# Odd layer's out projection: eight half-sized products become seven, with the sums of weight blocks made by transfers that add at their target

## The chip, the cores and the metric

The kernel runs on one core of one Trainium2 chip. The metric is the device time of one execution in microseconds (us); lower is better. Three runs of the kernel before stand at 1342.32, 1343.02 and 1346.22 us, median 1343.02.

## The reference, cut to what matters

Three transformer blocks run one after the other on 256 tokens of width 1024, all in f32: an even layer, an odd layer and a third block with 64 routed experts. The change touches the odd layer (index 1), from its attention outputs to the first layer norm:

```python
qf, kf, vf, fl = _split(x @ w_in_odd, ODD_SPLITS)
mix = forgetting_attention(hd(qf), hd(kf), hd(vf), fl, fox_f_bias) @ w_out_odd   # [256, 1024] @ [1024, 1024]
x = layer_norm(ALPHA * x + mix, ln_gain[1, 0], ln_bias[1, 0])
x = layer_norm(ALPHA * x + sqrelu_mlp(x, mlp_w_up[1], mlp_w_down[1]), ln_gain[1, 1], ln_bias[1, 1])
```

What is added up in `mix` must be the full product over all 1024 rows of `w_out_odd`.

## The kernel before, in words

Five engines run programs written out by hand, and semaphores order them. TensorE (`pe`) multiplies, VectorE (`dve`) takes products out of PSUM and normalises, ScalarE (`act`) does exponentials, square roots and copies, GpSimd (`pool`) issues a second stream of transfers and has a little arithmetic, and SyncE (`sp`) issues the stream of weights.

**Weights.** `d_stream` holds chunks of 1024 KB in the order of use. SyncE puts chunk n into slot n % 8 of `ring` as soon as chunk n - 8 is used (`s_used`, L675). The out projection's four chunks lie in slots 7, 0, 1 and 2. Each holds two row tiles of 128 rows by all 1024 columns. The first four chunks of the MLP behind it lie in slots 3 to 6, and its chunks 4 to 7 come into the slots 7, 0, 1, 2 once the out projection releases them.

**Out projection (`out_projection`, L984).** The attention outputs lie turned in `xT`: 8 tiles of 128 features by 256 tokens. Four quarters of the output (token tile t, column half) follow each other, each a sum of 8 matmuls 128x512 over the eight feature tiles, one PSUM bank each: 32 matmuls. Quarters 0 and 1 need token tile 0 of `xT` alone, quarters 2 and 3 need tile 1. Before the last quarter TensorE turns the normalised rows of token tile 0 (`turn_rows(x, "ln2", 0)`, L782).

**Residual (`residual`, L2333).** VectorE takes a quarter at a time, `y = ALPHA * x + ps`, and gathers its statistics (`half_stats`, L2256). After quarter 1 it normalises token tile 0 (`norm`, which is `layer_norm`, L2268 to L2274, with the square root by ScalarE) and then scales the context rows for the third block (`norm_context`, L2318 and L2323). After quarter 2 it copies half of the turned columns (`take_turn`, L2072) and makes two differences of MLP weight blocks (`other_differences`, L2503 and L2505). After quarter 3 it normalises token tile 1.

**MLP (`mlp(1)`).** Its up products begin with token tile 0's columns (L1002). In the middle of the second one TensorE turns the rows of token tile 1. It already uses seven products of halves in place of eight. Its down products (L1011) are each four matmuls 128x512, the same shape as a product of the change.

**GpSimd's queue** around the place, in order: gain and bias rows for both layer norms (`row`, L2972), a weight difference for the MLP (`first_difference`, L3008), the context load (L3148), a cleared row sum and three small bias loads (`start_sums`, L2993 and L2995), and two 1024 KB chunks of modulation weights (`start_mlp`, L3016), which VectorE reads during the MLP.

Of the kernel before, what the change touches and what calls it, by code (L numbers as in the profile page):

```python
# [19 lines left out]
ALU = mybir.AluOpType  # L20
# [28 lines left out]
HALF_SUMS = ODD_HALF + 4  # L49
DIFFS = ODD_DIFFS + 3 * 4  # L50
ADDED = ODD_ADDED + 3 * 6
TAKEN = ODD_TAKEN + 3

# [204 lines left out]
def build(nc, d_stream, d_params, d_consts, d_pool, d_x, d_ctx, d_gain, d_bias, d_ada, d_bada, d_final, d_out):  # L258
    with ExitStack() as ctx:
# [54 lines left out]
        s_fold = sem("fold_ready")  # L314
# [223 lines left out]
        def down_blocks(n0):  # L538

            chunks = [rows2(ring[:, (n0 + 4 + i) % RING, :]) for i in range(4)]  # L540
            return [[w[:, :, 512 * half:512 * (half + 1)] for w in chunks[2 * k:2 * k + 2]] for k in range(2) for half in range(2)]
        mod_sum = pairs[:].rearrange("p a b -> p (a b)")
# [227 lines left out]
        def _(pe):  # L770
# [177 lines left out]
            def mod_columns(n, tiles, bank):  # L948

                pe.wait_ge(s_fold, 1)  # L950
# [13 lines left out]
            def out_projection(n0, name, before_last):  # L964

                def wait_columns_of(t):
                    if name == "mix0":
                        wait_columns(name, t)
                    elif name == "mix1":
                        pe.wait_ge(s_odone, FIRST_TURNED + 2 * t + 2)  # L970
                    else:
                        pe.wait_ge(s_odone, FIRST_TURNED + 4 + t + 1)

                ws = [chunk(n0 + c).rearrange("p (k n) -> p k n", k=2) for c in range(4)]
                for q in range(4):
# [12 lines left out]
                    if q < 3:  # L988
                        mm.then_inc(s_quarter, 1)

            def mlp(layer, name, hook=None, before_last=None):
# [56 lines left out]
                def down(it, first=False, last=False):  # L1048
# [17 lines left out]
                    pe.wait_ge(s_y, it * 6 + (ADDED * layer + 1))  # L1066
# [3 lines left out]
                    pe.wait_ge(s_y, it * 6 + (ADDED * layer + 2))  # L1070
# [3 lines left out]
                    pe.wait_ge(s_y, it * 6 + (ADDED * layer + 3))  # L1074
# [72 lines left out]
            for c in range(2):  # L1147
# [7 lines left out]
                if c == 0:  # L1155
                    turn_hidden()
                    pe.wait_ge(s_fold, 1)
# [166 lines left out]
            out_projection(FIRST["out_odd"], "mix1", lambda: turn_rows(x, "ln2", 0))  # L1324
# [8 lines left out]
            pe.wait_ge(s_y, ADDED + ODD_ADDED)  # L1333
# [319 lines left out]
        def _(act):  # L1653
# [277 lines left out]
            for t in range(TT):  # L1931
                unread = (probT[:], hT[:, 0:4, :])[t].rearrange("p a b -> p (a b)")
# [126 lines left out]
        def _(dve):  # L2059
# [265 lines left out]
            def residual(section, before, norm, name, layer):  # L2325

                for q in range(4):
# [10 lines left out]
                    if q == 1 and layer == 1:  # L2338
                        norm_context()
                    if q == 2:  # L2340
                        take_turn(name, xT, only=0)
                        other_differences(layer)
# [28 lines left out]
            def mlp(layer, norm, hook=None, name=None):  # L2371
# [19 lines left out]
                def added(it, n):  # L2391
                    dve.wait_ge(s_y, it * 6 + (ADDED * layer + n))
# [99 lines left out]

            def other_differences(layer):
# [3 lines left out]
                if layer:  # L2497
                    dve.wait_ge(s_odone, FIRST_TURNED + 4)
                else:
                    dve.wait_ge(s_turn, TURN_AT["mix0"] + 4)  # L2500
                dve.wait_ge(s_full[(n0 + 2) % RING], 16 * ((n0 + 2) // RING + 1))
                dve.wait_ge(s_blk, 5 + layer)
# [823 lines left out]
```

## Time and profile before

| | before |
|---|---|
| median of 3 runs | 1343.02 us |
| the profiled execution's own time | 1343.69 us |
| its span in the profile | 1342.0 us |
| TensorE busy | 1319.2 us (98%) |
| VectorE busy | 678.5 us (51%) |
| ScalarE busy | 238.5 us (18%) |
| GpSimd busy | 95.8 us (7%) |
| out projection and its turn on TensorE | 487.15 to 515.60 us |
| moved from HBM | 356.88 MB, 267 GB/s over the span |

The profile is of one execution. Times count from the start of its span. The views used below are the page (totals and the chain of work that ended last), the timeline (instructions in order of time, neighbours of one kind merged), busy time by stretches, and the transfers with their time to landing. An f32 matmul of 128x512 shows as two records of 0.43 us each, so the 32 matmuls are 64 records. GpSimd's queue and SyncE's queue are served by the same 16 DMA engines.

### The profile page before, as it was taken

To read this page: it belongs to the slowest core of one execution; us is meant where nothing else is said; L and a number is where in the kernel's file an instruction comes from. 1 tells how busy PE (TensorE), PEld (TensorE's weight loads), DVE (VectorE), ACT (ScalarE), POOL (GpSimd) and SP (SyncE) were. 2 spreads that over 40 slices of the span, in tenths; PEclk is the share of its full clock that TensorE was granted. 3 is DMA by queue.
4 is the path that set the end of the run, shared out by engine and by line. 5 is a ranking of instruction groups with operands and counts; after the bars stand their busy time and mean duration, and the time that the engine had idled before them with its cause. 6 is when DMAs were issued, how large, how long until landed. Compare 5 with 4: busy or idle time off the path is not lost.

```text
span 1342.0 us, 19458 instructions
## 1 busy us (share of the span) xinstructions
PE 1319.2 (98%) x7520; PEld 821.6 (61%) x7520; DVE 678.5 (51%) x1261; ACT 238.5 (18%) x551; POOL 95.8 (7%) x116
## 2 busy tenths in 40 slices
PE   9999999999999999999999999999999999999996
PEld 8667585786789557588677666644444444444433
DVE  1235588877899549977887254322122122212213
ACT  2134321210220341120123152100000000000002
POOL 1125400000011030000000100000000000000001
PEclk9999999999999999999999999999999999999999
DMA  9930155555514445667664414499999999999994
GB/s 380 363 141 33 64 219 197 215 220 215 188 64 173 181 181 215 231 247 304 239 240 154 173 57 164 194 421 420 421 421 416 421 420 421 421 421 421 421 420 198
DMA packets 51072, 359.56 MB, mean 268 GB/s; under 512 B 5920, under 2 KB 6192, under 8 KB 8496
## 3 DMA queue, kind: packets, MB, share of 16 engines
q1 hardware_dynamic: 45312, 324.60, 60.1%
q0 software_dynamic: 5392, 32.05, 6.5%
q10 hardware_dynamic: 288, 1.80, 0.3%
q8 instruction: 56, 0.92, 0.3%
q14 instruction: 24, 0.20, 0.0%
HBM read 356.88 MB, written 1.05 MB: 267 GB/s over the span
## 4 chain that ended last, share of the span: by engine, by line
PE 91%; DVE 7%; issue 1%; ACT 0%; DVEq 0%; ACTq 0%
PE ps L1537 14%; PE ps L1011 13%; PE ps L1002 11%; PE ps L1566 7%; PE ps L1462 7%; PE ps L1515 7%; PE ps L984 5%; PE ps L819 4%; PE ps L1292 4%; PE ps L902 2%; PE ps L1285 2%; PE ps L923 2%; PE ps L824 1%; PE ps L858 1%; PE ps L1422 1%
## 5 line engine op out<-in xcount | busy, mean ns | idle before, releaser
L2845 DVE TENSOR_TENSOR masked_and_probs<-ps,gate_rows 128x512 f32<-128x512 f32 x52 | 33.5, 686 | 152.5 <-PE ps L1566 152.5
L1515 PE MATMUL ps<-masked_and_probs,probT 128*128 128x512 f32 x208 | 94.4, 594 | 0.9 <-DVE masked_and_probs L2845 0.9
L1462 PE MATMUL ps<-masked_and_probs,mix_rows 128*128 128x256 f32 (+1 forms) x416 | 93.0, 376 | 0.0
L1462 PEld LDWEIGHTS ps<-masked_and_probs,mix_rows 128*128 128x128 f32 x416 | 75.0, 190 | 28.8 <-issue 19.6
L1002 PEld LDWEIGHTS ps<-xT,ring 128*128 128x128 f32 x768 | 87.8, 192 | 3.8 <-issue 3.8
L1002 PE MATMUL ps<-xT,ring 128*128 128x128 f32 x768 | 88.7, 275 | 0.0
L1011 PE MATMUL ps<-ring,qk_tiles 128*128 128x512 f32 x192 | 85.2, 592 | 0.0
L984 PE MATMUL ps<-ring,xT 128*128 128x512 f32 x192 | 83.8, 593 | 0.0
L2833 DVE TENSOR_TENSOR masked_and_probs<-masked_and_probs,ps 128x256 f32<-128x256 f32 x26 | 11.0, 422 | 142.0 <-ACT masked_and_probs L2020 142.0
L1674 ACT ACTIVATE qk_tiles<-ps 128x512 f32<-128x512 f32 (+7 forms) x58 | 30.2, 522 | 246.2 <-PE ps L1002 238.5
L1537 PE MATMUL ps<-ring,vec_rows 128*32 128x512 f32 (+2 forms) x296 | 72.0, 592 | 0.0
L2020 ACT ACTIVATE masked_and_probs<-ps 128x256 f32<-128x256 f32 x26 | 10.0, 384 | 348.2 <-PE ps L1537 348.2
L1566 PE MATMUL ps<-ring,probT 128*32 128x512 f32 (+1 forms) x264 | 69.1, 596 | 0.1
L984 PEld LDWEIGHTS ps<-ring,xT 128*128 128x128 f32 x192 | 35.9, 190 | 42.9 <-issue 42.9
L1515 PEld LDWEIGHTS ps<-masked_and_probs,probT 128*128 128x128 f32 x208 | 37.2, 190 | 39.4 <-issue 39.1
L1011 PEld LDWEIGHTS ps<-ring,qk_tiles 128*128 128x128 f32 x192 | 35.8, 190 | 41.6 <-issue 41.1
L1002 PE MATMUL ps<-gate_rows,ring 128*128 128x128 f32 x512 | 59.9, 275 | 0.0
L1002 PEld LDWEIGHTS ps<-gate_rows,ring 128*128 128x128 f32 x512 | 58.4, 192 | 0.1
L1706 ACT ACTIVATE masked_and_probs<-masked_and_probs,negmax 128x128 f32<-128x128 f32 (+2 forms) x96 | 47.6, 497 | 59.4 <-DVE negmax L2232 52.1
L819 PE MATMUL ps<-xT,ring 128*128 128x256 f32 x240 | 52.7, 379 | 0.8 <-DVE xT L2072 0.8
L2357 DVE SCALAR_TENSOR_TENSOR masked_and_probs<-v_rows,csil,masked_and_probs 128x512 f32 (+1 forms) x64 | 48.0, 750 | 3.2 <-DMA v_rows<-in_ada 1.1
L819 PEld LDWEIGHTS ps<-xT,ring 128*128 128x128 f32 x240 | 45.2, 190 | 7.0 <-ACT xT L1662 1.0
(500 smaller groups left out, 2380.5 us busy)
## 6 DMA issues: line engine op xcount, KB each, us to landing
ring<-in_stream SPq DMA_DIRECT2D x200, 1024.0 KB, 9.7
qk_tiles<-in_stream SPq DMA_DIRECT2D x46, 1024.0 KB, 21.0
v_rows<-in_ada POOLq DMA_DIRECT2D x12, 1024.0 KB, 5.1
qk_tiles<-in_ada POOLq DMA_DIRECT2D x12, 1024.0 KB, 5.1
vec_rows<-in_stream SPq DMA_DIRECT2D x12, 1024.0 KB, 18.2
con<-in_stream SPq DMA_DIRECT2D x12, 1024.0 KB, 19.4
y_rows<-in_stream SPq DMA_DIRECT2D x12, 1024.0 KB, 20.4
par<-in_stream SPq DMA_DIRECT2D x12, 1024.0 KB, 21.1
```

The costliest lines, as they stand in the source:

```text
L819: mm = pe.matmul(ps[0:n, bank, off:off + T], w[:, kk, col:col + n], src[:, k, :], start=bank not in started, stop=k == KT - 1, skip_group_ ...
L984: mm = pe.matmul(ps[:, q, :], xT[:, k, t * P:(t + 1) * P], ws[k // 2][:, k % 2, half * 512:(half + 1) * 512], start=k == 0, stop=k == KT - 1)
L1002: mm = pe.matmul(ps[:, bank, m * P:(m + 1) * P], weights[:, kk, m * P:(m + 1) * P], tokens[:, kk, :], start=fresh and m == 0 and kk == 0, ...
L1011: mm = pe.matmul(ps[:, bank, :], hidden[:, kk, :], weights[kk // 2][:, kk % 2, :], start=fresh and kk == 0, stop=kk == 3, skip_group_check ...
L1292: mm = pe.matmul(ps[:, bank, m * P:(m + 1) * P], weights[:, kk, m * P:(m + 1) * P], tokens[:, kk, :], start=fresh and m == 0 and kk == 0, ...
L1462: mm = pe.matmul(ps[:, 5 + kk // 2, kk % 2 * 2 * P:kk % 2 * 2 * P + width], h2[:, t, k * P:(k + 1) * P], select[:, t, 0:width], start=t == ...
L1515: mm = pe.matmul(ps[:, q, :], probT[:, buf, 256 + q // 2 * P:256 + (q // 2 + 1) * P], yslot[:, q % 2 * 512:(q % 2 + 1) * 512], start=False ...
L1537: mm = pe.matmul(ps[cols, 4, :], rows[c][:, kk, cols], ws[a][:, kk, :], start=k == 0, stop=k == KT - 1, skip_group_check=True)
L1566: mm = pe.matmul(ps[lo:lo + width, 5 + half, :], probT[:, buf, k * P + lo:k * P + lo + width], ws[a][:, k, half * 512:(half + 1) * 512], s ...
L1706: act.activation(prob[:, u % 4, 0:nk], masked[:, u % 4, 0:nk], ACT.Exp, bias=negmax[:, u:u + 1], scale=-1.0, accum_out=esum[:, u:u + 1]).t ...
L2357: dve.scalar_tensor_tensor(out=at, in0=mod_slot[c % 2][:, kk, :], scalar=csil[:, 4 * (c % 2) + kk, cond:cond + 1], in1=at, op0=ALU.mult, o ...
L2845: dve.tensor_tensor(yslot[:, cols], ps[:, 5 + half, :], gaterow[:, 1, cols], ALU.mult).then_inc(ready, 1)
```

## The change

Both operands of the product are cut into halves: tokens (q1x, q2x), features (x1, x2) and columns. With `q11, q12` the two feature halves of token tile 0, `q21, q22` those of tile 1, and `b11, b12, b21, b22` the blocks of the weights, the program makes

- S1 = q21 - q22, S2 = S1 - q11, S3 = q12 + S2, S4 = q11 - q21 on VectorE, in `probT` and over q21 in `xT`;
- U1 = b12 + b11, U3 = b22 + b12, U2 = b11 + U3, U4 = b21 + U2, by transfers on GpSimd's queue with `accum_op=ALU.add`;
- seven products of four matmuls 128x512 each: q11 b11, q12 b21, S1 U1, S2 U2, S3 b22, S4 U3, q22 U4.

Several products are added up in one bank, with VectorE taking an intermediate value out between them. `out_odd` replaces `residual`. The two MLP differences move forward in it, the scaling of the context rows moves ahead of the first normalisation, and ScalarE's order of the two square roots follows. Two of the four gain and bias rows are loaded later, since their place holds U2. Four of the twelve transfers are plain (the first terms of U3 and U2), eight add at their target; all are of 512 KB. The remaining edits rename a semaphore and shift counts.

TensorE from the out projection to the turn of token tile 1, before (L984 out projection, L782 turns, L1002 MLP):

```order
L984 MATMUL ps<-ring,xT 128x512 [waits slot_full2,slot_full1,outs_taken,slot_full0,slot_full7]
L984 MATMUL ps<-ring,xT 128x512 x15
L984 MATMUL ps<-ring,xT 128x512 [waits outs_taken]
L984 MATMUL ps<-ring,xT 128x512 x7
L782 MATMUL ps<-con,x_rows 128x128 [waits rows_ready]
L782 MATMUL ps<-con,x_rows 128x128 x7
L984 MATMUL ps<-ring,xT 128x512 x8
L1002 MATMUL ps<-xT,ring 128x128 [waits slot_full3,xT_by_dve,xT_by_act]
```

and of the change (L1014 out projection, L797 turns, L1055 MLP; `probT` holds S1 to S3, `vec_rows` U2, `gate_rows` U3):

```order
L1014 MATMUL ps<-ring,xT 128x512 [waits slot_full2,slot_full1,outs_taken,slot_full0,slot_full7]
L1014 MATMUL ps<-ring,xT 128x512 x7
L1014 MATMUL ps<-ring,probT 128x512 [waits weight_sums_by_dma,token_half_sums]
...
L1014 MATMUL ps<-vec_rows,probT 128x512 [waits down_products_added,weight_sums_by_dma,token_half_sums]
...
L1014 MATMUL ps<-ring,probT 128x512 [waits down_products_added,token_half_sums]
...
L1014 MATMUL ps<-gate_rows,xT 128x512 [waits down_products_added,token_half_sums]
...
L1014 MATMUL ps<-ring,xT 128x512 [waits weight_sums_by_dma]
L1014 MATMUL ps<-ring,xT 128x512 x2
L797 MATMUL ps<-con,x_rows 128x128 [waits rows_ready]
L797 MATMUL ps<-con,x_rows 128x128 x7
L1014 MATMUL ps<-ring,xT 128x512
L1055 MATMUL ps<-xT,ring 128x128 [waits slot_full3,xT_by_dve,xT_by_act]
```

Each of the five products from the third on begins with a wait for `token_half_sums`, `weight_sums_by_dma` or both, and the turn now stands before the last matmul rather than before the last eight.

VectorE in the second half of the same place, of the change (L2559 adds a bank, L2309 statistics, L2327 end of a normalisation, L2554 first take, L2125 copy of the turned columns):

```order
L2327 SCALAR_TENSOR_TENSOR x_rows<-y_rows,small,vec_rows 128x1024 [waits dve_chain]
L2559 TENSOR_TENSOR y_rows<-y_rows,ps 128x512 [waits product_quarters_psum,rows_ready]
L2309 BN_STATS small<-y_rows 128x6 [waits dve_chain]
L2554 SCALAR_TENSOR_TENSOR y_rows<-x_rows,ps 128x512
L2125 COPY xT<-ps 128x4x128 [waits turned_psum,dve_chain]
L2559 TENSOR_TENSOR y_rows<-y_rows,ps 128x512 [waits chunks_used]
L2309 BN_STATS small<-y_rows 128x6 [waits dve_chain]
```

Between the normalisation of token tile 0 and the copy there were the context scaling, one take and one statistic; now there are two takes and one statistic, and the two differences of 128x2048 have left this place.

GpSimd's queue of the change from the modulation weights on:

```order
L3126 DMA v_rows<-in_ada 128x2048
L3126 DMA qk_tiles<-in_ada 128x2048
L3285 DMA ring<-vec_rows 128x2x512 [waits slot_full1,weight_sums_by_dma,product_quarters_psum]
L3285 DMA ring<-vec_rows 128x2x512 [waits slot_full2]
L3082 DMA vec_rows<-in_gain 128x1024 [waits product_quarters_psum,weight_sums_by_dma]
```

The two transfers that finish U4 stand behind both modulation chunks and wait for product 2, the last reader of b21; nothing stood between those chunks and the loop before.

The diff, cut to its core:

```diff
+            def out_products(n0, name, before_last):
+
+                b11, u1, b21, b22 = out_blocks(n0)
+                u4, before = b21, BEFORE_OUT["odd"]
...
+                pe.wait_ge(s_odone, FIRST_TURNED + 2)
+                product(quarters(xT, 0, 0), b11, 0, True).then_inc(s_quarter, 1)
+                product(quarters(xT, 0, 1), b21, 2, True).then_inc(s_quarter, 1)
+
+                pe.wait_ge(s_half, OUT_HALF + 1)
+                pe.wait_ge(s_wsum, 96)
+                product(out_s1, u1, 1, True).then_inc(s_used, 2)
+
+                pe.wait_ge(s_half, OUT_HALF + 2)
+                pe.wait_ge(s_wsum, 160)
+                pe.wait_ge(s_y, ADDED + 1)
+                product(out_s2, out_u2, 0, False).then_inc(s_quarter, 1)
+
+                pe.wait_ge(s_half, OUT_HALF + 4)
+                pe.wait_ge(s_y, ADDED + 2)
+                product(out_s3, b22, 1, False).then_inc(s_quarter, 1)
+
+                pe.wait_ge(s_half, OUT_HALF + 3)
+                pe.wait_ge(s_y, ADDED + 3)
+                product(out_s4, out_u3, 0, False).then_inc(s_quarter, 1)
+
+                pe.wait_ge(s_wsum, 192)
+                product(quarters(xT, 1, 1), u4, 3, True, before_last).then_inc(s_used, 2)
...
-            out_projection(FIRST["out_odd"], "mix1", lambda: turn_rows(x, "ln2", 0))
+            out_products(FIRST["out_odd"], "mix1", lambda: turn_rows(x, "ln2", 0))
...
-            std(0)
             act.wait_ge(s_ss, 1)
             std()
+            std(0)
...
+            def out_odd(norm, name):
...
+                dve.wait_ge(s_odone, FIRST_TURNED + 4)
+                dve.tensor_tensor(out_s1, q21, q22, ALU.subtract).then_inc(s_half, 1)
+                dve.wait_ge(s_half, OUT_HALF + 1)
+                dve.tensor_tensor(out_s2, out_s1, q11, ALU.subtract).then_inc(s_half, 1)
+                dve.wait_ge(s_half, OUT_HALF + 2)
+                dve.tensor_tensor(out_s4, q11, q21, ALU.subtract).then_inc(s_half, 1)
+
+                dve.wait_ge(s_quarter, before + 1)
+                first(0, 0, 0).then_inc(s_y, 1)
+                second()
+                dve.wait_ge(s_quarter, before + 2)
+                dve.wait_ge(s_y, ADDED + 1)
+                link(add(0, 0, 2))
+                half_stats(0)
+                third()
+                dve.wait_ge(s_used, used_before + 2)
+                first(1, 1, 1).then_inc(s_y, 1)
+                dve.tensor_tensor(out_s3, q12, out_s2, ALU.add).then_inc(s_half, 1)
+                norm_context()
+                dve.wait_ge(s_quarter, before + 3)
+                first(0, 1, 0, ALU.subtract).then_inc(s_y, 1)
+                dve.wait_ge(s_quarter, before + 4)
+                dve.wait_ge(s_y, ADDED + 3)
+                link(add(0, 1, 1))
+                half_stats(1)
+                norm(0)
+                dve.wait_ge(s_quarter, before + 5)
+                link(add(1, 1, 0, ALU.subtract))
+                half_stats(3, False)
+                link(first(1, 0, 0))
+                take_turn(name, xT, only=0)
+                dve.wait_ge(s_used, used_before + 4)
+                link(add(1, 0, 3))
+                half_stats(2, True)
+                norm(1)
...
+            pool.wait_ge(s_prod, odd_product(2, 6))
+            pool.wait_ge(s_diff, DIFFS)
+            for i in range(2):
+                pool.dma_start(out_u3[i], stored(2 + i, 1)).then_inc(s_wsum, 16)
+                pool.dma_start(out_u2[i], stored(i, 0)).then_inc(s_wsum, 16)
+            for i in range(2):
+                n = FIRST["out_odd"] + i
+                pool.wait_ge(s_full[n % RING], 16 * (n // RING + 1))
+                pool.dma_start(u1[i], stored(i, 0), accum_op=ALU.add).then_inc(s_wsum, 16)
+            pool.wait_ge(s_wsum, 96)
+            for i in range(2):
+                pool.dma_start(out_u3[i], stored(i, 1), accum_op=ALU.add).then_inc(s_wsum, 16)
+            pool.wait_ge(s_wsum, 128)
+            for i in range(2):
+                pool.dma_start(out_u2[i], out_u3[i], accum_op=ALU.add).then_inc(s_wsum, 16)
+
             pool.wait_ge(s_y, ADDED)
             row(vec[:, 0, :], d_gain[1, 0:1, :], s_vecA)
             row(vec[:, 2, :], d_bias[1, 0:1, :], s_vecA)
-            row(vec[:, 1, :], d_gain[1, 1:2, :], s_vecB)
-            row(vec[:, 3, :], d_bias[1, 1:2, :], s_vecB)
...
             start_mlp(1)
+            pool.wait_ge(s_quarter, BEFORE_OUT["odd"] + 2)
+            pool.wait_ge(s_wsum, 160)
+            for i in range(2):
+                n = FIRST["out_odd"] + 2 + i
+                pool.wait_ge(s_full[n % RING], 16 * (n // RING + 1))
+                pool.dma_start(u4[i], out_u2[i], accum_op=ALU.add).then_inc(s_wsum, 16)
+            pool.wait_ge(s_wsum, 192)
+            pool.wait_ge(s_quarter, BEFORE_OUT["odd"] + 3)
+            row(vec[:, 1, :], d_gain[1, 1:2, :], s_vecB)
+            row(vec[:, 3, :], d_bias[1, 1:2, :], s_vecB)
```

`product` issues four matmuls, the last-named argument being called before the fourth; `first` is `ALPHA * x` with a bank added (or subtracted), `add` adds a bank to `y`; `second` and `third` are the two parts of `other_differences`. `FIRST_TURNED` is 9, so the first wait is for token tile 0's outputs.

## Rows read from the trace of the kernel before

**Rows 1.** The page, parts 1 and 4: totals, and the chain that ended last.

```profile
PE 1319.2 (98%) x7520; PEld 821.6 (61%) x7520; DVE 678.5 (51%) x1261; ACT 238.5 (18%) x551; POOL 95.8 (7%) x116
...
PE 91%; DVE 7%; issue 1%; ACT 0%; DVEq 0%; ACTq 0%
```

**Rows 2.** Timeline, TensorE, 487 to 524: start us, us, engine, line, records, [idle before].

```profile
487.15 3.27 PE L984 MATMUL ps<-ring,xT 128*128 128x512 f32 x7
...
507.86 1.04 PE L782 MATMUL ps<-con,x_rows 128*128 128x128 f32 x8
508.73 7.03 PE L984 MATMUL ps<-ring,xT 128*128 128x512 f32 x16
515.60 5.52 PE L1002 MATMUL ps<-xT,ring 128*128 128x128 f32 x48
521.44 1.09 PE L782 MATMUL ps<-con,x_rows 128*128 128x128 f32 x8 [0.32 <-DVE x_rows L2274]
```

**Rows 3.** Timeline, two products of four matmuls 128x512 in the MLP.

```profile
608.85 3.60 PE L1011 MATMUL ps<-vec_rows,qk_tiles 128*128 128x512 f32 x8
612.28 3.60 PE L1011 MATMUL ps<-ring,qk_tiles 128*128 128x512 f32 x8
```

**Rows 4.** Timeline, VectorE around the out projection.

```profile
487.26 0.69 DVE L2136 TENSOR_TENSOR xT<-ps,mix_rows 128x512 f32<-128x512 f32 x1 [0.84 <-PE ps L858]
494.32 0.69 DVE L2333 SCALAR_TENSOR_TENSOR y_rows<-x_rows,ps 128x512 f32<-128x512 f32 x1 [6.37 <-PE ps L984]
501.91 0.69 DVE L2256 BATCH_NORM_STATS2 small<-y_rows 128x6 f32<-128x512 f32 x1
505.23 1.28 DVE L2274 SCALAR_TENSOR_TENSOR x_rows<-y_rows,small,vec_rows 128x1024 f32<-128x1024 f32 x1
506.55 0.17 DVE L2318 TENSOR_SCALAR small<-small 128x2 f32<-128x2 f32 x1
508.04 1.54 DVE L2323 TENSOR_SCALAR qk_tiles<-qk_tiles,small 128x1024 f32<-128x1024 f32 x2
510.96 0.67 DVE L2072 COPY xT<-ps 128x512 f32<-128x512 f32 x1
511.55 2.28 DVE L2503 TENSOR_TENSOR mix_rows<-ring 128x2048 f32<-128x2048 f32 x1
516.07 0.68 DVE L2333 SCALAR_TENSOR_TENSOR y_rows<-x_rows,ps 128x512 f32<-128x512 f32 x1
523.37 0.69 DVE L2364 TENSOR_TENSOR gate_rows<-xT 128x512 f32<-128x512 f32 x1
```

**Rows 5.** Timeline, GpSimd and SyncE's queue: issues and GpSimd's own work.

```profile
459.54 3.26 SPq L675 DMA_DIRECT2D ring<-in_stream  x4
468.73 4.68 POOL L3008 TENSOR_TENSOR ring<-ring 128x1024 f32<-128x1024 f32 x2 [4.84 <-DMA ring<-in_stream]
488.25 0.75 POOL L3148 DMA_DIRECT2D qk_tiles<-in_ctx  x1 [14.84 <-DVE xT L2136]
494.83 0.54 POOL L3016 DMA_DIRECT2D qk_tiles<-in_ada  x1
510.79 18.33 SPq L675 DMA_DIRECT2D ring<-in_stream  x6
```

**Rows 6.** Busy time by stretches: us, PE, PEld, DVE, ACT, POOL, PEclk, DMA share, GB/s.

```profile
444.00:447.00 3.00, 3.00 (x9) 1.33 (x8) 0.41 (x4) 0.00 (x0) 0.00 (x0) 1.00 0.00 0
...
498.00:500.00 2.00, 2.00 (x6) 0.94 (x5) 0.00 (x0) 0.00 (x0) 0.00 (x0) 1.00 1.02 426
500.00:502.00 2.00, 2.00 (x6) 0.91 (x5) 0.78 (x2) 0.00 (x0) 0.00 (x0) 1.00 0.56 238
502.00:504.00 2.00, 2.00 (x7) 0.80 (x6) 1.93 (x4) 0.20 (x1) 0.00 (x0) 1.00 0.00 0
```

**Rows 7.** Transfers of `in_ada` (three, 425 to 540): issue to landing.

```profile
DMA to landing us min/median/max: 5.0/7.0/8.0
```

**Rows 8.** Transfers of `in_gain` (four, 512 KB each, whole span): issue to landing.

```profile
DMA to landing us min/median/max: 8.1/11.1/15.3
```

More of the change, by code:

```diff
@@ L48 @@
 PRODS = ODD_PRODS + 3 * 6
-HALF_SUMS = ODD_HALF + 4
+OUT_HALF = ODD_HALF + 4
+HALF_SUMS = OUT_HALF + 4
 DIFFS = ODD_DIFFS + 3 * 4
 ADDED = ODD_ADDED + 3 * 6
+MLP_ADDED = ADDED + 3
 TAKEN = ODD_TAKEN + 3
+BEFORE_OUT = {"even": 0, "odd": 3, "2": 8}
 MOD_VECTORS = ((0, 1), (2, 5, 3, 4))
@@ L541, in down_blocks, with out_blocks @@
             return [[w[:, :, 512 * half:512 * (half + 1)] for w in chunks[2 * k:2 * k + 2]] for k in range(2) for half in range(2)]
+        def out_blocks(n0):
+            chunks = [rows2(ring[:, (n0 + i) % RING, :]) for i in range(4)]
+            return [[w[:, :, 512 * half:512 * (half + 1)] for w in chunks[2 * k:2 * k + 2]] for k in range(2) for half in range(2)]
+        out_u2 = [rows2(vec[:, 1 + 2 * i, :]) for i in range(2)]
+        out_u3 = [rows2(gaterow[:, i, :]) for i in range(2)]
+        out_s1, out_s2, out_s3 = block4(probT[:, 0, :]), block4(probT[:, 1, :]), block4(probT[:, 0, :])
+        out_s4 = quarters(xT, 1, 0)
         mod_sum = pairs[:].rearrange("p a b -> p (a b)")
@@ L989, in out_projection, with product @@
                         mm.then_inc(s_quarter, 1)
+            def out_products(n0, name, before_last):
+                b11, u1, b21, b22 = out_blocks(n0)
+                u4, before = b21, BEFORE_OUT["odd"]
+                def product(rows, weights, bank, fresh, within=None):
+                    for kk in range(4):
+                        if within and kk == 3:
+                            within()
+                        mm = pe.matmul(ps[:, bank, :], rows[:, kk, :], weights[kk // 2][:, kk % 2, :],
+                                       start=fresh and kk == 0, stop=kk == 3, skip_group_check=True)
+                    return mm
+                for c in range(4):
+                    chunk(n0 + c)
+                pe.wait_ge(s_odone, FIRST_TURNED + 2)
[16 more added lines that the diff above has]
+                product(quarters(xT, 1, 1), u4, 3, True, before_last).then_inc(s_used, 2)
             def mlp(layer, name, hook=None, before_last=None):
@@ L2337, in residual @@
                         norm(q // 2)
-                    if q == 1 and layer == 1:
-                        norm_context()
                     if q == 2:
                         take_turn(name, xT, only=0)
-                        other_differences(layer)
+                        for difference in other_differences(layer):
+                            difference()
             def modulate(layer, it, piece):
@@ L2491, in mlp, with first, add @@
                 norm(1)
+            def out_odd(norm, name):
+                before, used_before = BEFORE_OUT["odd"], FIRST["out_odd"]
+                second, third = other_differences(1)
+                q11, q12, q21, q22 = (quarters(xT, t, half) for t in range(TT) for half in range(2))
+                at = lambda t, half: (slice(None), t, slice(half * 512, (half + 1) * 512))
+                def first(t, half, bank, op=ALU.add):
+                    return dve.scalar_tensor_tensor(out=y[at(t, half)], in0=x[at(t, half)], scalar=ALPHA, in1=ps[:, bank, :],
+                                                    op0=ALU.mult, op1=op)
+                def add(t, half, bank, op=ALU.add):
+                    return dve.tensor_tensor(y[at(t, half)], y[at(t, half)], ps[:, bank, :], op)
+                dve.wait_ge(s_odone, FIRST_TURNED + 4)
[32 more added lines that the diff above has]
+                norm(1)
```

50 lines of the change are left out of this document (27 added, 23 removed).

## The prediction, made before the change was run

> **What bounds the kernel now.** I read the page first: TensorE is busy 1319.2 of 1342.0 us, and the chain of work that ended last runs 91% over it [rows 1]. So a matmul taken away counts, if TensorE does not wait in its place. Then the timeline of the place. TensorE runs through it without a gap: the first six half-quarters of four matmuls take 487.15 to 507.86 (20.71 us for 24 matmuls), the turn of token tile 0 stands to 508.73, the last quarter to 515.60, and the MLP's up products follow at once. Its only wait is 0.32 us at 521.44, for the normalised rows of token tile 1 [rows 2]. I take this start at 521.44 as the yardstick: whatever it moves by, the rest moves by, since the MLP, the third block and its loads start from work that follows it. Last come the transfers: the engines are idle before 447 and again from about 501 to 511, full from 498 to 500 [rows 6].
>
> **What is removed.** 32 matmuls become 28. Six groups of four take 20.71 us, 3.45 each [rows 2]; the MLP's products of the same shape start 3.43 us apart (608.85, 612.28) [rows 3]. So the change takes away **3.45 us** of TensorE. This is also its ceiling. About 4.0 us (0.3%) is what a measurement of this kernel can tell from no change.
>
> **TensorE after, if nothing is late.** Products 1 to 7 start at 487.15, 490.60, 494.05, 497.51, 500.96, 504.41 and 507.86. Product 7 starts where the turn starts now. The turn (0.87 us) comes after three of its matmuls: 510.45 to 511.32; the last matmul ends at 512.18.
>
> **VectorE's terms.** The last columns of token tile 1 are written at 487.26 + 0.69 = 487.95; S1, S2, S4 cost 0.69 each, the row of a 128x512 sum of two SBUF operands, so they are done at 490.0, S1 needed at 494.05 [rows 4]. An intermediate bank is free 0.31 + 0.69 us after its product (the first take of before starts 0.31 us after 494.01) [rows 2, 4]. Then, with 2.3 us for each moved difference [rows 4]: take 490.9 to 491.6; first difference to 493.9; add, statistic and second difference 494.4 to 498.1; take of product 3 to 498.8; S3 at 499.5, needed at 500.96; the context scaling, 506.55 to 509.58 now, so 3.03 us, to 502.5 [rows 4]; the take of product 4 to 503.2, needed by product 6 at 504.41. The closest margin is 1.2 us. Add and statistic of product 5: the statistic starts at 505.4. From the statistic (501.91) to normalised rows (505.23 + 1.28) there are 4.60 us [rows 4], so token tile 0 is ready at 510.0, needed by the turn at 510.45. Only 0.4 us is left, but nothing waits.
>
> **What becomes late.** Behind that normalisation VectorE has a take, a statistic and another take (2.1 us) before it copies the turned columns: 512.2 to 512.9. TensorE has ended at 512.18, and the up product starts at 513.0: **0.8 us idle**. Before, the copy (510.96) lay beside the last quarter. 5.52 us of up product and turn wait later [rows 2], at 518.5, TensorE wants token tile 1's rows. VectorE's last add starts at 512.9 and, as from 516.07 to 521.44 now [rows 2, 4], the rows come 5.37 us later, 518.3. So the yardstick moves from 521.44 to 518.5: **-2.9 us** with no late transfer. (TensorE saves 3.45, loses 0.8, and the 0.32 of now goes.)
>
> **The early transfers.** Eight of the twelve can go from 448.4 on, when `gate_rows` is free (U3, U2 plain; U1), then by waits the adds into U3 and U2. Engines are idle there [rows 6]; U1 is needed at 494.05, U2 at 497.51. Even if each of the six adds took the slowest landing of a 512 KB row load (15.3 us [rows 8]), in three groups one after another, they would end before 448.4 + 5 + 3 x 15.3 = 499; overlap inside the groups and the plain rate bring that to about 470. I cost them at nothing. They share the engines with SyncE's four loads at 459.54, on which GpSimd's difference waits now (468.73 to 473.4) [rows 5]; it is needed by VectorE at 491.6, so about 18 us of cover. If the sums held GpSimd's queue beyond that, the context load (488.25) and the modulation chunks would slip too.
>
> **The late transfers: U4.** Product 2 releases b21 at 494.05, but GpSimd is at its two modulation chunks until 495.37 [rows 5]. So the two adds into U4 are issued at 495.4 and about 496.2, behind 2048 KB in the same queue. Now those 2048 KB end at about 501.1 (full to 500, 0.56 of the next 2 us, nothing after) [rows 6]. New beside them: product 3 releases slots 7 and 0 at about 497.7, and SyncE at once issues two loads of 1024 KB, which before came at 510.79 [rows 5]. At 426 to 428 GB/s [rows 6] 1024 KB take 2.45 us of full engines, so the two loads 4.9 us. U4 is 1024 KB written. Its price is not shown by any row: **at the plain rate** it takes 2.45 us, and the queue is empty at 501.1 + 4.9 + 2.45 = 508.5; **at half the plain rate** (an add must fetch its target as well as its source) 4.9 us, 510.9. The chunks now land up to 8.0 us after their issue at 494.3 [rows 7], thus 502.3, about 1.0 us after the last byte. So U4 lands between 509.5 and 511.9, against a need at 507.86. The slowest row of GpSimd's queue under SyncE's loads, 15.3 us [rows 8], gives 496.2 + 15.3 = 511.5, the same end. If instead U4 did not have to share with the two loads it would land at 501.1 + 2.45 + 1.0 = 504.6, in time. Less than nothing it can't cost.
>
> With product 7 starting at S, later than 507.86, it ends at S + 4.32, and the yardstick, 5.84 us after that as now (515.60 to 521.44 [rows 2]), is S + 10.16. S = 509.5 gives 519.7 (-1.8 us); S = 511.9 gives 522.1 (+0.6 us). I take the middle, 510.7, since the rows don't say which end the add is nearer to: 520.9, **-0.6 us**.
>
> The Trainium skill speaks against this change (Collectives: The Full Stack, "The bandwidth ceiling: the fold count and why AG ≠ RS ≠ AR"): an adding transfer needs two source reads and so runs at half the rate of a copy, though the addition itself is free. By it the sum would be +0.6 us in place of -0.6; no transfer of the kernel before adds, so no row here shows it.
>
> **Sum.** The profiled execution took 1343.69 us, 0.67 above the median of the runs, 1343.02. -0.6 gives 1343.1 on its scale and **1342.4 us** for the median. Most of the 3.45 us go into a wait of TensorE before product 7 (2.8 us) and the later copy.
>
> **Rivals.**
> *U4 is in time* (its packets are not slowed by SyncE's loads, or these move later). For it: the engines are free from 501.1 on now [rows 6]. Against it: in the one stretch where both queues were full, GpSimd's 512 KB loads took 8.1 to 15.3 us to land, where the full rate would need 1.2 each [rows 8]. It gives -2.9 us, **1340.1**.
> *The add runs at exactly half rate and last*, the skill's rule above as a mechanism of this kernel: U4's 4.9 us come after everything else, S = 511.9, +0.6 us, **1343.6**.
> *Slower: adding transfers are much slower than copies.* The place is again product 7, which waits in TensorE's queue with the turn and the whole MLP behind it. The loss is 4 us at S = 521.44 + 4.0 - 10.16 = 515.3; with 1.0 us for landing and the two loads done, that is 8.3 us of transfer for U4, 3.4 times the plain rate's. At four times (9.8 us) S = 516.8, +5.5 us, **1348.5**. At eight times the early sums would end near 517 too, and product 4 would wait 20 us. For it: nothing in the trace shows an add, and pieces are 2 KB where chunks move in 8 KB. Against it: engines idle between 501 and 511 give a wide allowance.
> *Faster than the ceiling*, by something outside this place (the two differences of VectorE that leave the busy start of the MLP): TensorE shows no wait there apart from 0.32 us [rows 2], so hardly.
>
> **Chances.** Forecast (S from 509.5 to 511.5) 0.38; U4 in time or nearly 0.23; half rate or a little slower, up to +4 us, 0.21; much slower 0.14; faster than by 4 us 0.04. The forecast's own range is 1341.2 to 1343.4. For 8 in 10 I go from 1339.8 (in time, with 0.3 us for the scatter of runs) to 1346.6 (part of the slow case, S near 515). Bounds of 0.3%: faster 0.04, same 0.82, slower 0.14.
>
> **What the profile after should show.** The seven products as 56 records, each group 3.45 us apart from 487.15; products 3 to 6 without a wait; one wait before the seventh, its releaser a transfer into `ring` from `vec_rows`, 1.6 to 4 us long; SyncE's next two loads near 498; a gap of up to 1 us before the first up product, for VectorE's copy; the turn of token tile 1 at 520.9. The argument is wrong if products 3 to 6 wait (VectorE's order or the early sums), if GpSimd's difference or context load moves past 488, or if the product count shows and the turn still stands at 521 with no wait for a transfer: then something else took the time.

## The result and the profile after

The change made the kernel **slower by 0.39%**: ratio 1.0039, 95% interval 1.0027 to 1.0052, medians 1349.66 against 1344.21 us (six runs of each, those of before now including three more). The forecast was 1342.4 us, -0.6 us against the median known then, with a range up to 1346.6; measured were +5.2 us by the ratio. The point lies beyond the bound of 0.3% above which I had given a chance of 0.14; the interval reaches down to 0.27%.

The page of the kernel after, parts 1 and 4, answering to [rows 1]:

```profile
PE 1317.7 (98%) x7512; PEld 820.1 (61%) x7512; DVE 684.0 (51%) x1269; ACT 238.4 (18%) x551; POOL 107.7 (8%) x128
...
PE 91%; DVE 4%; DMA 2%; issue 1%; POOL 1%; ACT 0%; DVEq 0%; SPq 0%; ACTq 0%
PE ps L1590 13%; PE ps L1064 13%; PE ps L1055 12%; PE ps L1619 7%; PE ps L1515 7%; PE ps L1568 7%; PE ps L997 4%; PE ps L834 4%; PE ps L1345 4%; PE ps L917 2%; PE ps L1338 2%; PE ps L938 2%; DMA ring<-vec_rows 1%; PE ps L839 1%; PE ps L873 1%; PE ps L1475 1%
```

Eight matmul records are gone, four matmuls as intended. The chain of work that ended last now holds DMA, and names the transfer `ring<-vec_rows`: U4. TensorE in the timeline, answering to [rows 2]:

```profile
494.36 3.60 PE L1014 MATMUL ps<-ring,probT 128*128 128x512 f32 x8
497.79 3.60 PE L1014 MATMUL ps<-vec_rows,probT 128*128 128x512 f32 x8
501.23 3.60 PE L1014 MATMUL ps<-ring,probT 128*128 128x512 f32 x8
504.66 3.60 PE L1014 MATMUL ps<-gate_rows,xT 128*128 128x512 f32 x8
514.37 4.37 PE L1014 MATMUL ps<-ring,xT 128*128 128x512 f32 x6 [6.11 <-DMA ring<-vec_rows]
518.58 1.04 PE L797 MATMUL ps<-con,x_rows 128*128 128x128 f32 x8
519.45 1.02 PE L1014 MATMUL ps<-ring,xT 128*128 128x512 f32 x2
520.51 5.60 PE L1055 MATMUL ps<-xT,ring 128*128 128x128 f32 x48
525.94 1.05 PE L797 MATMUL ps<-con,x_rows 128*128 128x128 f32 x8
```

Products 3 to 6 follow each other 3.43 to 3.44 us apart without a wait. Before product 7 TensorE stands for 6.11 us. Then its first three matmuls (six records) take 514.37 to 518.58, 4.21 us where three take 2.57 elsewhere.

Product 1 starts up to 1.5 us apart from profile to profile (487.15 before, 487.39 here, 485.90 to 487.37 in the experiments). This comes from something ahead of the place: GpSimd's first transfer for the sums, issued at 448.96 here, goes out at 447.46 in the profile in which product 1 starts at 485.90. So I use one **yardstick** below: from the start of product 1 to the turn of token tile 1. It was 521.44 - 487.15 = **34.29 us** before and is 525.94 - 487.39 = **38.55 us** after: +4.3 of the 4.7 us by which the two spans differ.

VectorE in the timeline, answering to [rows 4]:

```profile
495.89 2.27 DVE L2613 TENSOR_TENSOR qk_tiles<-mix_rows,ring 128x2048 f32<-128x2048 f32 x1
498.68 0.69 DVE L2578 TENSOR_TENSOR probT<-xT,probT 128x512 f32<-128x512 f32 x1
502.35 0.69 DVE L2554 SCALAR_TENSOR_TENSOR y_rows<-x_rows,ps 128x512 f32<-128x512 f32 x1
508.91 1.28 DVE L2327 SCALAR_TENSOR_TENSOR x_rows<-y_rows,small,vec_rows 128x1024 f32<-128x1024 f32 x1
519.72 0.69 DVE L2125 COPY xT<-ps 128x512 f32<-128x512 f32 x1 [7.49 <-PE ps L797]
```

S3 is ready at 499.4 (needed 501.2), the take of product 4 at 503.0 (needed 504.7), token tile 0's rows at 510.2: VectorE is late nowhere, and at 512 to 519.7 it waits itself. GpSimd's queue, answering to [rows 5]:

```profile
451.85 2.29 POOL L3263 DMA_DIRECT2D ring<-in_stream  x2
463.91 2.19 POOL L3266 DMA_DIRECT2D gate_rows<-in_stream  x2 [9.77 <-DMA ring<-in_stream]
480.21 1.77 POOL L3269 DMA_DIRECT2D vec_rows<-gate_rows  x2 [14.11 <-DMA gate_rows<-in_stream]
483.15 4.67 POOL L3118 TENSOR_TENSOR ring<-ring 128x1024 f32<-128x1024 f32 x2
488.49 0.74 POOL L3277 DMA_DIRECT2D qk_tiles<-in_ctx  x1 [0.67 <-DVE xT L2189]
495.06 0.54 POOL L3126 DMA_DIRECT2D qk_tiles<-in_ada  x1
495.58 2.54 POOL L3285 DMA_DIRECT2D ring<-vec_rows  x2
514.62 0.59 POOL L3082 DMA_DIRECT2D vec_rows<-in_gain  x1 [16.49 <-DMA ring<-vec_rows]
```

The sums for U1 are seen at 463.9, those for U3 at 480.2; those for U2 are issued then and landed after 4.7 and 7.7 us, near 488.5 at the latest, against a need at 497.8. GpSimd's weight difference slips from 468.73 to 483.15 and ends 0.67 us ahead of the context load's moment, where GpSimd used to be idle for 14.84 us: still hidden, barely. The context load itself goes out 1.10 us after the start of product 1, as before. U4 is issued at 495.58 and seen at 514.4. SyncE's two loads went out at 498.13. Busy time by stretches, answering to [rows 6]:

```profile
504.00:506.00 2.00, 2.00 (x6) 0.81 (x5) 1.10 (x2) 0.00 (x0) 0.00 (x0) 1.00 1.06 345
...
510.00:512.00 2.00, 0.00 (x0) 0.00 (x0) 1.93 (x4) 0.00 (x0) 0.00 (x0) 0.66 1.13 218
512.00:514.00 2.00, 0.00 (x0) 0.00 (x0) 0.23 (x1) 0.00 (x0) 0.00 (x0) 0.50 0.29 51
514.00:516.00 2.00, 1.63 (x2) 0.84 (x3) 0.00 (x0) 0.00 (x0) 1.15 (x2) 0.50 0.10 14
516.00:518.00 2.00, 2.00 (x4) 0.86 (x3) 0.00 (x0) 0.00 (x0) 0.00 (x0) 0.63 0.90 307
518.00:520.00 2.00, 2.00 (x12) 1.21 (x10) 0.28 (x1) 0.60 (x1) 0.00 (x0) 1.00 0.60 203
```

Two things stand here that the rows of before did not have. With the engines full (share 1.13) only 218 GB/s are moved, against 426 for plain chunks [rows 6]. And the granted clock falls to 0.50, from 2.4 to 1.2 GHz, while TensorE stands idle (0.66 in the stretch from 510 to 512), and is back at 1.00 only in the stretch from 518: the first matmuls of product 7 ran at half speed.

### The profile page after: what moved, and what is told of

Its sections match the earlier page's. It is cut to its first block, busy times and chain, and to the rows that moved or that the text cites. A ratio compares the mean times of both kernels' runs of the same rounds, so it can differ in the third digit from the quotient of the medians.

```text
span 1346.7 us, 19472 instructions
## 1 busy us (share of the span) xinstructions
PE 1317.7 (98%) x7512; PEld 820.1 (61%) x7512; DVE 684.0 (51%) x1269; ACT 238.4 (18%) x551; POOL 107.7 (8%) x128
## 4 chain that ended last, share of the span: by engine, by line
PE 91%; DVE 4%; DMA 2%; issue 1%; POOL 1%; ACT 0%; DVEq 0%; SPq 0%; ACTq 0%
PE ps L1590 13%; PE ps L1064 13%; PE ps L1055 12%; PE ps L1619 7%; PE ps L1515 7%; PE ps L1568 7%; PE ps L997 4%; PE ps L834 4%; PE ps L1345 4%; PE ps L917 2%; PE ps L1338 2%; PE ps L938 2%; DMA ring<-vec_rows 1%; PE ps L839 1%; PE ps L873 1%; PE ps L1475 1%
## 5 line engine op out<-in xcount | busy, mean ns | idle before, releaser
L1055 PEld LDWEIGHTS ps<-xT,ring 128*128 128x128 f32 x768 | 87.7, 192 | 4.2 <-issue 3.3
L1055 PE MATMUL ps<-xT,ring 128*128 128x128 f32 x768 | 88.8, 275 | 0.0
L1055 PE MATMUL ps<-gate_rows,ring 128*128 128x128 f32 x512 | 59.9, 275 | 0.0
L1055 PEld LDWEIGHTS ps<-gate_rows,ring 128*128 128x128 f32 x512 | 58.4, 192 | 0.1
L997 PE MATMUL ps<-ring,xT 128*128 128x512 f32 x128 | 55.9, 593 | 0.0
L2409 DVE SCALAR_TENSOR_TENSOR masked_and_probs<-qk_tiles,csil,masked_and_probs 128x512 f32 (+1 forms) x64 | 48.0, 750 | 1.7
## 6 DMA issues: line engine op xcount, KB each, us to landing
par<-in_stream SPq DMA_DIRECT2D x12, 1024.0 KB, 20.7
```

Source lines behind the costliest of these rows:

```text
L997: mm = pe.matmul(ps[:, q, :], xT[:, k, t * P:(t + 1) * P], ws[k // 2][:, k % 2, half * 512:(half + 1) * 512], start=k == 0, stop=k == KT - 1)
L1055: mm = pe.matmul(ps[:, bank, m * P:(m + 1) * P], weights[:, kk, m * P:(m + 1) * P], tokens[:, kk, :], start=fresh and m == 0 and kk == 0, ...
L2409: dve.scalar_tensor_tensor(out=at, in0=mod_slot[c % 2][:, kk, :], scalar=csil[:, 4 * (c % 2) + kk, cond:cond + 1], in1=at, op0=ALU.mult, o ...
```

## The experiments

Theory A: only U4's lateness costs, made up of its place in the queue behind the modulation chunks, SyncE's two loads beside it and the price of the add; the clock is a further loss that follows from standing idle. Rivals: the new order on VectorE and the early sums cost something by themselves; or an add is slow wherever it stands. Intervals are of the ratio to the kernel before, run on the same chip; the experiments ran on two chips, so two of them are compared by their ratios.

Besides what the views show, the traces record every packet that the DMA engines moved, with its queue, size, start and duration. U4's adds are 512 packets of 2 KB there, U4's copies 256 of 4 KB, the modulation chunks and SyncE's loads packets of 8 KB. Figures called "by the packets" are from these records.

**U4 left out**, and the wait for it; the kernel then leaves the sum out of its result:

```diff
-                pool.dma_start(u4[i], out_u2[i], accum_op=ALU.add).then_inc(s_wsum, 16)
-                pe.wait_ge(s_wsum, 192)
```

> The two adds into U4 are left out and product 7 waits for no transfer (it multiplies by b21 instead of U4, so this part of the result is left out). Yardstick: from the start of product 1 to the turn of token tile 1, 34.3 us before and 38.6 us with the change. Theory (only U4's lateness costs): no wait before product 7, clock full, yardstick about 31.4 us, time 2.5 to 3.5 us under the kernel before, ratio 0.998. Rival (VectorE's new order or the early sums cost something by themselves): yardstick 33 us or more, ratio 1.000 or above.

Measured: yardstick 517.25 - 486.16 = 31.09 us, ratio 0.9970 (0.9958 to 0.9983). The full loss hangs on U4. VectorE's order and the ten early transfers cost nothing on this path.

**U4 ahead of the modulation chunks.**

```diff
-            start_mlp(1)
             pool.wait_ge(s_quarter, BEFORE_OUT["odd"] + 2)
...
+            start_mlp(1)
```

> The two adds into U4 are issued before the two modulation chunks. Theory (U4 was late because it stood behind 2048 KB in its queue): issue near 494.5, landing 503 to 508, no wait or one under 0.5 us before product 7, yardstick 31.4 to 31.9 us, ratio to the kernel before 0.998. Rival (an add next to other traffic takes some 16 us to land wherever it stands in the queue): landing near 511, wait of 3 us or more, clock falls, yardstick 34.5 us or more, ratio 1.000 or above.

Measured: ratio **0.9972 (0.9962 to 0.9982)**, median 1341.11 against 1343.95 us. Its timeline of TensorE and of GpSimd:

```profile
486.20 7.13 PE L1014 MATMUL ps<-ring,xT 128*128 128x512 f32 x16
...
506.91 2.74 PE L1014 MATMUL ps<-ring,xT 128*128 128x512 f32 x6
509.48 1.04 PE L797 MATMUL ps<-con,x_rows 128*128 128x128 f32 x8
510.36 1.02 PE L1014 MATMUL ps<-ring,xT 128*128 128x512 f32 x2
511.87 5.60 PE L1055 MATMUL ps<-xT,ring 128*128 128x128 f32 x48 [0.49 <-issue]
517.30 1.04 PE L797 MATMUL ps<-con,x_rows 128*128 128x128 f32 x8
```

```profile
493.64 2.53 POOL L3284 DMA_DIRECT2D ring<-vec_rows  x2 [0.32 <-PE ps L1014]
495.19 1.58 POOL L3126 DMA_DIRECT2D v_rows<-in_ada  x1
...
506.61 0.53 POOL L3082 DMA_DIRECT2D vec_rows<-in_gain  x1 [9.28 <-DMA ring<-vec_rows]
```

Product 7 follows without a wait; yardstick 31.10 us, as with U4 left out. GpSimd sees the landing at 506.61, 20.4 us after product 1's start; product 7 starts at 20.7. It fits by 0.3 us. The modulation chunks land later for it, up to 18.4 us after their issue, and TensorE does not wait for them in this place. The rival (some 16 us wherever it stands) falls: the adds landed 11.9 us after their issue at most. Nothing moved from the kernel of the change but one block of lines, and it beats both kernels.

**SyncE's two loads held back** until product 7 (VectorE's signal for product 3 goes over another semaphore):

```diff
-                product(out_s1, u1, 1, True).then_inc(s_used, 2)
+                product(out_s1, u1, 1, True).then_inc(s_quarter, 1)
...
-                product(quarters(xT, 1, 1), u4, 3, True, before_last).then_inc(s_used, 2)
+                product(quarters(xT, 1, 1), u4, 3, True, before_last).then_inc(s_used, 4)
```

> Product 3 no longer releases the slots 7 and 0; all four chunks are released at product 7, so that SyncE's two loads do not run beside U4. Theory (U4 shared the engines with these 2048 KB, 4.9 us): modulation chunks end near 501, the adds alone at about 207 GB/s end near 506.5, landing near 508, wait under 1 us, yardstick 31.5 to 32.3 us, ratio 0.998. Rival (the queue order or the add alone is the cause, the loads are not): landing after 511, wait over 3 us, yardstick 35 us or more.

Measured: product 7 starts at 508.76, 21.6 us after product 1 (27.0 with the change), a wait of 0.73 us, the clock stays at 1.00, yardstick 518.81 - 487.16 = 31.65 us; ratio 0.9991 (0.9981 to 1.0000). The two loads cost U4 5.4 us; I had put 4.9. Here the adds run alone:

```profile
502.00:504.00 2.00, 2.00 (x6) 0.81 (x5) 0.78 (x2) 0.00 (x0) 0.00 (x0) 1.00 1.02 211
504.00:506.00 2.00, 2.00 (x6) 0.95 (x5) 1.33 (x2) 0.00 (x0) 0.00 (x0) 1.00 1.12 204
```

With full engines 204 GB/s in the second row (211 in the first, where by the packets the last of the modulation chunks still moves), half the 426 of a chunk: 1024 KB (1049 thousand bytes) take 5.1 us. The change's own trace agrees: 207 GB/s from 458 to 462, where U1's adds run.

**U4 by plain copies**, at the same place in the queue; the kernel leaves b21 out of product 7:

```diff
-                pool.dma_start(u4[i], out_u2[i], accum_op=ALU.add).then_inc(s_wsum, 16)
+                pool.dma_start(u4[i], out_u2[i]).then_inc(s_wsum, 16)
```

> The two transfers into U4 copy U2 instead of adding it (b21 is left out of this product). Same bytes written, same place in the queue. Theory (the add costs 5 us or more where a copy costs 2.45): data end near 508.7 to 509.5, landing near 510, wait of 1.5 to 2.5 us, yardstick 32.5 to 33.5 us, ratio 0.999 to 1.000. Rival (adds cost no more than copies, the queue alone is late): wait near 6 us as with the change, yardstick 38 us, ratio 1.004.

```profile
510.22 5.49 PE L1014 MATMUL ps<-ring,xT 128*128 128x512 f32 x6 [3.14 <-DMA ring<-vec_rows]
...
508.00:510.00 2.00, 0.00 (x0) 0.00 (x0) 1.93 (x3) 0.00 (x0) 0.00 (x0) 0.80 0.19 76
...
514.00:516.00 2.00, 2.00 (x6) 0.86 (x5) 0.00 (x0) 0.00 (x0) 0.00 (x0) 0.50 0.37 152
516.00:518.00 2.00, 1.96 (x12) 1.16 (x11) 1.00 (x2) 0.60 (x1) 0.00 (x0) 1.00 0.00 0
```

Product 7 starts 510.22 - 486.22 = 24.0 us after product 1, 3.0 us sooner than with adds: the add's price over a copy's. The wait is 3.14 us, not 1.5 to 2.5, since I had placed the landing too early even for copies. The yardstick, 523.12 - 486.22 = 36.90 us, is far over what was expected: this wait of half the length also brought the clock down, and product 7's first three matmuls took 510.22 to 515.51, 5.3 us. By yardstick = product 7's start + 10.16 it would be 34.2 us at full clock, so the clock took 2.7 us here, more than with the longer wait of the change. The rows show why: with copies the clock stood at 0.50 up to 516, and TensorE worked from 510.22 on; with the change it fell later, and TensorE worked only from 514.37 on before it rose between 516 and 518. Ratio 1.0008 (0.9998 to 1.0018); this is one profile, and whether it is typical stays open.

**Six idle-time matmuls** ahead of the wait, into an unused bank, to keep TensorE busy:

```diff
+                for _ in range(6):
+                    pe.matmul(ps[:, 7, :], ident, con[:, 0:512], start=True, stop=True)
                 pe.wait_ge(s_wsum, 192)
```

> As the change, with six matmuls 128x512 into an unused bank between product 6 and the wait for U4 (5.2 us of the 6.1 us that TensorE stood idle); their result is never read. Theory (the granted clock fell because TensorE stood idle, and product 7 and the turn then ran slow): U4 lands as late as before, near 27 us after the start of product 1, but the clock stays at 1.00, three matmuls of product 7 take 2.6 us and not 4.2, yardstick 38.6 - 1.6 = 36.9 us, ratio 1.002 to 1.003. Rival (the clock would fall anyway, or the loss is the wait alone): yardstick 38.5 us, ratio 1.004.

```profile
506.70 5.31 PE L1042 MATMUL ps<-con 128*128 128x512 f32 x12
512.91 2.84 PE L1014 MATMUL ps<-ring,xT 128*128 128x512 f32 x6 [0.89 <-DMA ring<-vec_rows]
```

Product 7 starts 512.91 - 486.00 = 26.9 us after product 1, as late as with the change (27.0), but the clock stays at 1.00 and the yardstick is 522.96 - 486.00 = 36.96 us: 1.6 us of the change's loss are the clock. Ratio 1.0023 (1.0012 to 1.0034); this overlaps the change's interval (1.0027 to 1.0052), so the gain rests on the profiles, where the clock and the start of product 7 can be read.

**U4 early, and the copy of the turned columns ahead of VectorE's take.**

```diff
-                link(first(1, 0, 0))
                 take_turn(name, xT, only=0)
+                link(first(1, 0, 0))
```

> U4's adds ahead of the modulation chunks, and VectorE copies the turned columns before its take of quarter (1,0), not after it. Theory (the copy delays the first up product by 0.65 us, but token tile 1's normalisation is then the next to be late, and it moves back by the same take): gap before the up products falls to about 0.2 us, the normalised rows come 0.3 us later, TensorE waits for them instead, yardstick 31.0 to 31.4 us as with U4 early alone, no difference in time. Rival (the gap is all that is left to win): yardstick 30.6 us, 0.5 us faster than U4 early alone.

```profile
511.08 5.59 PE L1055 MATMUL ps<-xT,ring 128*128 128x128 f32 x48
516.99 1.09 PE L797 MATMUL ps<-con,x_rows 128*128 128x128 f32 x8 [0.32 <-DVE x_rows L2327]
```

The gap ahead of the up products (0.49 us with U4 early) is gone, and TensorE waits 0.32 us for token tile 1's rows in its place: yardstick 516.99 - 485.94 = 31.05 us, ratio 0.9979 (0.9970 to 0.9988). A gain given back 6 us later. After this edit VectorE's chain from product 7 to the normalised rows is what TensorE waits for.

**U4 by GpSimd's own arithmetic**, two sums of 128x1024 in place of the adds, ahead of the modulation chunks:

```diff
-                pool.dma_start(u4[i], out_u2[i], accum_op=ALU.add).then_inc(s_wsum, 16)
+                pool.tensor_tensor(u4[i], u4[i], out_u2[i], ALU.add).then_inc(s_blk, 1)
```

> U4 is made by GpSimd's own arithmetic (two sums of 128x1024, 2.35 us each as its weight difference) in place of two adding transfers, ahead of the modulation chunks. Theory (only U4's arrival matters): U4 ready near 12 us after the start of product 1, against 20.7 needed, no wait, yardstick 31.1 us, ratio 0.997, equal to U4 early within 0.1%. Rival (GpSimd and VectorE, which makes a difference of 128x2048 at the same time, slow each other): VectorE's difference takes over 2.6 us, S3 or the take of product 4 comes late, products 5 or 6 wait, yardstick 32 us or more.

```profile
494.43 6.73 POOL L3284 TENSOR_TENSOR ring<-ring,vec_rows 128x1024 f32<-128x1024 f32 x2
495.71 3.24 DVE L2613 TENSOR_TENSOR qk_tiles<-mix_rows,ring 128x2048 f32<-128x2048 f32 x1
499.48 2.24 DVE L2578 TENSOR_TENSOR probT<-xT,probT 128x512 f32<-128x512 f32 x1
501.77 3.70 PE L1014 MATMUL ps<-ring,probT 128*128 128x512 f32 x8 [0.56 <-DVE probT L2578]
```

Here the rival's mechanism shows. Beside GpSimd's sums VectorE's difference takes 3.24 in place of 2.27 us and S3 2.24 in place of 0.69, GpSimd's own two sums 6.73 in place of 4.7; product 5 waits 0.56 us, and product 6 starts 3.76 us after it in place of 3.43. Yardstick 519.13 - 487.21 = 31.92 us, nearly the 32 at which I had put the rival. The time still is 0.9977 (0.9969 to 0.9986), not to be told from U4 early (0.9962 to 0.9982). U4 was ready long before product 7, so GpSimd's arithmetic is another way, with a larger margin for U4 and a smaller one for VectorE.

**The price of the add and of the loads, with U4 early**: one kernel holds SyncE's loads back as above, one copies as above and so leaves b21 out. One run each, 1340.47 and 1340.35 us, beside one of the kernel before at 1345.87; they are read by their profiles alone.

> U4's adds ahead of the modulation chunks, and SyncE's two loads held back to product 7. With U4 early alone the engines moved only about 180 GB/s from 496 to 502, no more than U4 itself, although two loads had been issued at 497. Theory (adds keep the engines to themselves, the loads beside them take nothing from them): U4 takes the same 5 to 6 us of data and TensorE and GpSimd see it at the same time, about 20.2 us after the start of product 1. Rival (the loads did take a share): U4 lands 1 us or more sooner, under 19.2 us.

> U4's transfers ahead of the modulation chunks, but as plain copies (b21 is left out of product 7). Theory (an add costs a little over twice a copy on the engines, 5.0 against 2.45 us for 1024 KB): GpSimd sees them landed about 3 us sooner than as adds, 17 to 17.7 us after the start of product 1. Rival (it is the issue and the landing that take long, not the data): under 1 us sooner, 19.2 us or later.

The timeline of GpSimd and, below it, the landing of U4's two transfers, with the loads held:

```profile
493.34 2.53 POOL L3284 DMA_DIRECT2D ring<-vec_rows  x2 [0.30 <-PE ps L1014]
...
502.64 0.54 POOL L3082 DMA_DIRECT2D vec_rows<-in_gain  x1 [5.60 <-DMA ring<-vec_rows]
...
DMA to landing us min/median/max: 5.3/6.8/8.2
```

and as copies:

```profile
494.80 1.51 POOL L3284 DMA_DIRECT2D ring<-vec_rows  x2 [0.31 <-PE ps L1014]
...
DMA to landing us min/median/max: 3.2/4.0/4.8
```

Held: seen landed 502.64 - 485.90 = 16.7 us after product 1, 3.7 us sooner than with the loads beside it. My theory here (the loads take nothing) is wrong, although the engines moved the same 180 GB/s or so in both. The total over 16 engines hides how far each of them is, and a transfer has landed only with its last part. By the packets this is the reason: 500 of the 512 packets had ended 16.2 us after the start of product 1 with the loads and 15.7 us with the loads held, but the last one 19.5 against 16.1 us. So the loads cost the bulk of U4 0.5 us and its last 12 packets 3.3 us. The very last ones end 0.48 us apart, as they would if their engine moved an 8 KB packet (0.31 us) between two of them (0.18 us each); that is an estimate from the durations. Copies: issued in 1.51 us for both where adds take 2.53, and landed 495.6 + 4.8 = 500.4, 13.0 us after product 1's start, against 20.4 as adds. That is more than the 3 us expected: next to the loads an early add loses twice, by its own data and by being still under way when they begin.

## Why the prediction was wrong

**Right.** The matmuls taken away (3.43 to 3.45 us) and that nothing in products 3 to 6 waits. The terms of VectorE. The gap by the later copy: forecast 0.8, measured 0.65 us counted as the forecast counts (510.36 + 0.86 to 511.87 with U4 early), 0.49 us by the timeline. The case without a late transfer: -2.9 us forecast, 31.10 - 34.29 = -3.2 us measured. That U4 waits before product 7, and what it queues behind.

**The step that failed is U4's landing, S.** I placed product 7 at 510.7, 23.55 us after product 1, between 22.35 (plain rate) and 24.8 (half rate). Measured were 26.98, 3.4 us more. Copies in the same place came at 24.0, so the add cost 3.0 us over a copy, where I had put 1.2 by taking the middle of two ends and 2.45 by the upper end. The other 1.6 us have nothing to do with adding. The packets show where they and the rest lie, counted from the start of product 1:

| | forecast | copies | change |
|---|---|---|---|
| modulation chunks ended | 13.95 | 14.9 | 15.3 |
| then both loads and U4, without its last packets | 8.6 (copies: 7.35) | 7.35 | 10.0 |
| then U4's last packets (2 of 256, 12 of 512) | 0 | 0.9 | 1.3 |
| from the last packet to product 7 | 1.0 | 0.8 | 0.4 |
| product 7 starts | 23.55 (copies: 22.35) | 24.0 | 27.0 |

The second row is the price of the add. For the copies my sum was exact; with the 4.9 us of the two loads taken off, the adds took 5.1 us, the upper end (4.9), where the sum had 3.7. The "middle" had no row behind it. The first and third rows are terms that I had too small or at nothing: the chunks ended later (14.3 by the packets even before the change; why they lose up to 1 us more with it is open), and the 16 engines do not end together.

**Readings of rows that were wrong.** The 8.0 us to landing [rows 7] belong to the third chunk, issued at 529.84; the two of this place took 5.0 and 7.0, which gives 501.8 and 0.7 us in place of 1.0. The 15.3 us [rows 8] belong to a load at 36.7 us; those next to SyncE's loads at 462 took 8.1 and 13.7, so "the same end", 511.5, had no support. Ten of the twelve transfers go early, not eight. The bound of 499 for the early sums lay behind the need at 494.05 and 497.51 and could not show that they cost nothing. And "the context load past 488" was no sign of anything, since it stood at 488.25 before.

**The rule that I weighed was the better guide.** The Trainium skill (Collectives: The Full Stack, "The bandwidth ceiling: the fold count and why AG ≠ RS ≠ AR") states for a reduce-scatter against an all-gather that the add halves the rate because it needs two source reads. The runs here agree on the rate: 204 GB/s for adds that run alone against 426 for chunks. That two reads are the cause no run here shows. With the half rate my sum would have been +0.6 us, still 3.7 us short: the rest is the first and third rows above and the next item.

**A second step failed, a term that was missing: the clock.** I costed the wait at its length. Its 6.1 us of idle time took the granted clock to 0.50, and the first three matmuls of product 7 ran into it (4.21 us in place of 2.57): 1.6 us, isolated by the filled wait (38.55 - 36.96). The formula "yardstick = S + 10.16" holds with the clock at 1.00 (26.91 + 10.16 = 37.07 against 36.96 with the wait filled) and misses by 1.4 us in the change (37.14 against 38.55). Sum of the yardstick's error: 3.4 (landing) + 1.4 = 4.8 us, which is the difference between 33.7 forecast and 38.55 measured.

**Mis-sized without effect: the early sums.** I had them ended near 470 with 18 us of cover for GpSimd's difference. U1's and U3's were seen at 463.9 and 480.2, U2's landed near 488.5, and 14.4 of the 18 us were used. Costing them at nothing was right, but by 0.67 us of slack in GpSimd's queue.

**The rival on the slow side** (product 7 as the place, 4 us of loss from S = 515.3 on) had the place right and the price wrong: the loss came at S = 514.4, with adds at half rate, not at under a third. The clock made up the difference: a start of product 7 that would have cost 2.8 us cost 4.3.

## What to carry to other kernels

A transfer that adds at its target is not free because no engine computes it: count twice its bytes on the DMA engines, a longer issue, everything that is queued ahead of it or released beside it, and that its last packets can end well after the rest; and put it ahead of transfers that nobody waits for yet. A wait of TensorE for a few microseconds costs more than its length once the granted clock falls; where the wait can't be removed, work that keeps TensorE busy gets part of it back. When a step's price has no row, don't take the middle: take the end for which there is a mechanism.

## What the runs showed of the hardware that was not expected

- The granted clock fell during a wait of 3.14 us (copies) as during one of 6.11 us (the change), and with the change stayed at 0.50 until 516 and into the stretch from 516 to 518, through product 7's matmuls. It did not fall at waits of 0.73 us (loads held) and 0.89 us (wait filled). The shorter wait lost more by the clock, 2.7 us against 1.4 to 1.6, since more of TensorE's work fell into the slow stretch.
- Issuing two adds took GpSimd 2.53 us, two copies of the same shape 1.49 to 1.51, one modulation chunk 0.54.
- By the packets, an add's 2 KB packet took 0.18 us and a copy's 4 KB packet, of the same tensors, 0.16. Adds alone moved 204 GB/s over the 16 engines; the copies would come to some 410, an estimate from that duration.
- With U4 early, SyncE's loads were issued at 496.9, but by the packets almost nothing of them moved before 501.2. Until 502 the engines moved 127 to 195 GB/s at a share of 1.06 to 1.14, and the adds landed 3.7 us later than with the loads held, by their last packets.
- GpSimd's and VectorE's sums of two SBUF operands slowed each other: 0.69 us became 2.24 for S3 while GpSimd summed beside it, and GpSimd's own two sums took 6.73 us in place of 4.67.
